# Attention probabilities, the last mixer part and x turned by 32-wide squares; the first two output blocks interleaved

## The reference

```
GLA(h) * silu(g_a)        gated linear attention, 4 heads
SSD(h, g_b)               state space mixer, 8 heads, gated and normed inside
MLA(h) * silu(g_c)        causal softmax attention, 4 heads of 192/128
DilatedSWA(h) * silu(g_d) softmax attention over dilated taps, 4 heads of 128
y = concat of the four, 256 x 2048;  x = x + y @ W_out (2048 x 2048)
```

## Time and profile before

| | |
|---|---|
| median of 3 runs | 809.48 us (809.12 to 809.54) |
| the profiled execution, its own time | 809.36 us |
| its span, first to last instruction | 807.6 us |
| busy: PE, DVE, ACT, POOL | 801.6, 616.7, 469.0, 100.5 us |
| granted TensorE clock | 0.999 |
| weights, queue q1 | 149.98 MB, 57.9% of 16 engines' span |
| POOL's queue, q0 | 18.95 MB, 8.6% |
| HBM over the span | 209 GB/s |

### The profile page before, as it was taken

The page is one execution under the profiler, slowest core; times in us unless marked ns, Lnnn a source line. Parts: engine busy times, 40 slices in busy tenths (PEclk is TensorE's granted clock), DMA queues, the critical chain, the costliest instruction groups (busy, mean ns, idle before and its releaser), DMA issues.

```text
span 807.6 us, 10773 instructions
## 1 busy us (share of the span) xinstructions
PE 801.6 (99%) x3940; PEld 678.9 (84%) x3940; DVE 616.7 (76%) x1084; ACT 469.0 (58%) x762; POOL 100.5 (12%) x154
## 2 busy tenths in 40 slices
PE   8999999999999999999999999999999999999998
PEld 5888888999887888888888888889998888888886
DVE  6678899887898776678964967988779988765452
ACT  6666544857865667443556465447777566663431
POOL 6200000030432211000000000002105231100000
PEclk9999999999999999999999999999999999999999
DMA  9966544576697977655676645365757979766663
GB/s 328 348 221 210 182 131 155 168 248 188 210 290 234 280 203 235 209 186 182 185 250 185 195 155 195 107 188 169 234 190 240 271 239 284 217 193 213 188 193 117
DMA packets 51348, 169.82 MB, mean 210 GB/s; under 512 B 6688, under 2 KB 7376, under 8 KB 51296
## 3 DMA queue, kind: packets, MB, share of 16 engines
q1 hardware_dynamic: 44736, 149.98, 57.9%
q0 software_dynamic: 6240, 18.95, 8.6%
q10 hardware_dynamic: 320, 0.21, 0.1%
HBM read 157.56 MB, written 11.55 MB: 209 GB/s over the span
## 4 chain that ended last, share of the span: by engine, by line
PE 91%; DVE 6%; issue 2%; DMA 1%; SPq 0%; ACT 0%; DVEq 0%
PE gemm L750 27%; PE gemm L741 27%; PE gemm L742 27%; DVE arena L1381 3%; DVE w_lo L1420 2%; PE pairs L917 1%; DMA raw<-in_weights_dram 1%; PE pairs L896 1%; PE pairs L891 1%; PE pairs L892 1%; PE pairs L862 1%; PE pairs L807 1%; DVE arena L1509 1%; PE pairs L931 1%; PE pairs L944 0%
## 5 line engine op out<-in xcount | busy, mean ns | idle before, releaser
L1420 DVE TENSOR_TENSOR w_lo<-raw,w_hi 128x1024 fp32r<-128x1024 f32 (+2 forms) x279 | 323.0, 1169 | 143.2 <-ACT w_hi L1046 142.3
L741 PE MATMUL gemm<-w_hi,a_hi 128*128 128x512 f32 (+2 forms) x1080 | 415.0, 384 | 0.8 <-ACT w_hi L1046 0.8
L742 PE MATMUL gemm<-w_hi,a_lo 128*128 128x512 f32 (+2 forms) x1080 | 408.9, 379 | 0.0
L1046 ACT ACTIVATE w_hi<-raw 128x1024 fp32r<-128x1024 f32 (+2 forms) x279 | 278.5, 1012 | 209.3 <-PE gemm L750 127.2
L750 PE MATMUL gemm<-w_lo,a_hi 128*128 128x512 f32 (+2 forms) x1080 | 278.4, 379 | 0.2
L741 PEld LDWEIGHTS gemm<-w_hi,a_hi 128*128 128x128 f32 x1080 | 202.8, 188 | 36.8 <-ACT w_hi L1046 1.7
L742 PEld LDWEIGHTS gemm<-w_hi,a_lo 128*128 128x128 f32 x1080 | 203.0, 188 | 33.4
L750 PEld LDWEIGHTS gemm<-w_lo,a_hi 128*128 128x128 f32 x1080 | 199.4, 188 | 36.7 <-DVE w_lo L1420 2.2
L634 POOL TENSOR_TENSOR st<-st,powers 128x4 f32<-128x4 f32 (+2 forms) x8 | 2.5, 309 | 365.5 <-ACT arena L1127 213.0
L1079 ACT ACTIVATE u<-gemm,st 128x512 f32<-128x512 f32 (+2 forms) x36 | 21.3, 646 | 15.3 <-PE gemm L750 15.3
L1381 DVE STREAM_TRANSPOSE arena<-u 32x256 f32<-32x256 f32 x64 | 27.9, 436 | 1.2
(11 more groups left out here) (215 smaller groups left out, 663.0 us busy)
## 6 DMA issues: line engine op xcount, KB each, us to landing
raw<-in_weights_dram SPq DMA_DIRECT2D x225, 512.0 KB, 4.2
raw<-in_weights_dram SPq DMA_DIRECT2D x38, 384.0 KB, 3.5
raw<-in_weights_dram SPq DMA_DIRECT2D x16, 344.0 KB, 3.5
y_squares<-arena POOLq DMA_DIRECT2D x6, 512.0 KB, 5.8
arena<-y_squares POOLq DMA_DIRECT2D x24, 128.0 KB, 5.8
x<-in_x_dram SPq DMA_DIRECT2D x4, 512.0 KB, 6.0
o<-ssd_rows SPq DMA_DIRECT2D x8, 256.0 KB, 5.3
param_rows<-in_params_dram SPq DMA_DIRECT2D x2, 904.0 KB, 8.0
```

The costliest lines, as they stand in the source:

```text
L741: pe.matmul(acc_t[t], a_hi[:, k, tok[t]], hi, start=k == 0, stop=False)
L742: pe.matmul(acc_t[t], a_lo[:, k, tok[t]], hi, start=False, stop=False)
L1046: A_(w_hi[:, g % SPLIT, 0:c], raw[:, g % RAW, 0:c], ACT.Copy).then_inc(hi_done, 1)
L1420: TT(w_lo[:, g % SPLIT, 0:c], raw[:, g % RAW, 0:c], w_hi[:, g % SPLIT, 0:c].bitcast(F32), ALU.subtract).then_inc(split_done, 1)
```

## The change

- `probs_T` and `yT` are gone from PE, with their four plus one jobs a layer. After `mla P i` and `dil P i` DVE makes squares of the probabilities (`probs_squares`, two transposes), POOL sends them out and back (384 KB each way), and ACT's `probs_T` reorders them into `PT`. The buffer is the finished `dq`/`dk` part of `u`, one token half for each i.
- The values go behind slots 98, 102, 107 and 112; ACT's copy to `PT` stands one slot on.
- `y 3` goes by squares as the other three.
- The stream visits output blocks 13 and 14 as six units of 13, six of 14, then the last two of 13 and of 14. Only those last need `yT 3`, whose copy moves to slot 125. The sums into x of the two blocks move to slots 128 and 130 (from 122 and 130).
- Quarters 0 to 2 of x go by squares (two DVE transposes each) at slots 129, 131 and 139; ACT's and DVE's splits read them in another order, DVE in two instructions per 128 features for one.
- POOL's list gets the new transfers in a fixed order.

```diff
+TAIL = UPB - 2
+FIRST_OUT = [U_OUT + b * UPB + k for k0, k1 in ((0, TAIL), (TAIL, UPB)) for b in range(2) for k in range(k0, k1)]
-for _n in range(UNITS):
+for _n in [*range(U_OUT), *FIRST_OUT, *range(U_OUT + 2 * UPB, UNITS)]:
...
-          "mla kv 1": KV_AT, "ssd Y": 76, "mla rT": 87, "mla S 0": 90, "mla PT 0": 93,
-          "mla S 1": 94, "mla O 0": 95, "mla PT 1": 97, "mla O 1": 99, "dil S 0": 99,
-          "dil PT 0": 102, "dil S 1": 103, "dil O 0": 104, "dil PT 1": 106, "dil O 1": 108,
-          "yT 3": 114}
+          "mla kv 1": KV_AT, "ssd Y": 76, "mla rT": 87, "mla S 0": 90,
+          "mla S 1": 94, "mla O 0": 98, "dil S 0": 99, "mla O 1": 102, "dil S 1": 103, "dil O 0": 107, "dil O 1": 112}
...
-Y_TURN = {1: 98, 0: 100, 2: 107}
-Y_SPLIT = [110, 112, 114, 117]
+Y_TURN = {1: 98, 0: 100, 2: 107, 3: 115}
+Y_SPLIT = [110, 112, 114, 125]
-X_NEXT = {N_SLOTS - 21: 0, N_SLOTS - 13: 1, N_SLOTS - 5: 2}
+X_NEXT = {N_SLOTS - 15: 0, N_SLOTS - 13: 1, N_SLOTS - 5: 2}
+X_UPDATE = {N_SLOTS - 16: N_INB, N_SLOTS - 14: N_INB + 1, N_SLOTS - 6: N_INB + 2}
...
+        for _i in range(2):
+            SQUARES[f"mla P {_i}"] = SQUARES[f"dil P {_i}"] = (u[:, _i, COL["dq"]:COL["dq"] + 768],) * 2 + ((94, 98)[_i],)
+        for _j, _n in zip(X_NEXT.values(), X_NEXT):
+            SQUARES[f"x {_j}"] = (u[:, 0, _j * 1024:(_j + 1) * 1024],) * 2 + (_n,)
...
                 squares_back(l, "ssd y")
                 squares_out(l, "dil q")
+                squares_out(l, "dil k")
+                squares_out(l, "mla P 0")
                 rsqrt("ssd rs", brs, bss)
-                squares_out(l, "dil k")
+                squares_back(l, "mla P 0")
                 squares_back(l, "dil q")
                 squares_back(l, "dil k")
-                for name in ("y 1", "y 0", "y 2"):
+                squares_out(l, "mla P 1")
+                squares_back(l, "mla P 1")
+                squares_out(l, "y 1")
+                squares_out(l, "dil P 0")
+                squares_back(l, "y 1")
+                squares_back(l, "dil P 0")
+                for name in ("y 0", "dil P 1", "y 2"):
                     squares_out(l, name)
                     squares_back(l, name)
 
+                squares_out(l, "y 3")
+                squares_back(l, "y 3")
+                if l + 1 < DEPTH:
+                    for j in range(3):
+                        squares_out(l, f"x {j}")
+                        squares_back(l, f"x {j}")
                 pool.wait_ge(*reached("dve", l)("yT 3"))
 
...
-                def yT(j):
-
-                    pe.wait_ge(*dve(f"y {j}"))
-                    ps = bank()
-                    for kk in range(4):
-                        for t in range(T):
-                            f = kk * P
-                            last = pe.transpose(ps[:, kk // 2, (kk % 2) * S + t * P:(kk % 2) * S + (t + 1) * P], o[:, j, t, f:f + P], ident)
-                    last.then_inc(*signal("pe", f"yT {j}"))
...
-                def probs_T(m, i):
-
-                    pe.wait_ge(*(act if m == "mla" else dve)(f"{m} P {i}"))
-                    ps = bank()
-                    for r in range(2):
-                        for c in range(3):
-                            last = pe.transpose(ps[:, r, c * P:(c + 1) * P], Pb[:, r, c * P:(c + 1) * P], ident)
-                    last.then_inc(*signal("pe", f"{m} PT {i}"))
...
                 def probs_T(m, i):
-                    act_.wait_ge(*pe(f"{m} PT {i}"))
-                    A_(PT[:, :, :], pair_of(f"{m} PT {i}")[:, :, 0:384], ACT.Copy).then_inc(*signal("act", f"{m} PT {i}"))
+                    act_.wait_ge(squares_in[f"{m} P {i}"], 16 * 4 * (l + 1))
+                    if (m, i) != ("mla", 0):
+                        act_.wait_ge(*pe(f"{m} O 0" if i else "mla O 1"))
+                    to, squares = PT.rearrange("p r (c i a) -> p i (r c) a", i=4, a=32), SQUARES[f"{m} P {i}"][1].rearrange("p (i x a) -> p i x a", i=4, a=32)
+                    A_(to, squares, ACT.Copy).then_inc(*signal("act", f"{m} PT {i}"))
...
-                                if n == slot(f"{m} PT {i}"):
+                                if n == slot(f"{m} O {i}", 1):
                                     probs_T(m, i)
...
+                    if l and i < len(X_NEXT):
+                        for t in range(T):
+                            hi, lo = (tokens(m[:, k, :])[:, t] for m in (a_hi, a_lo))
+                            last = v.scalar_tensor_tensor(lo, turned(i, k)[:, t], gain(l, k), hi.bitcast(F32), ALU.mult, ALU.subtract)
+                        continue
...
-                    if i:
-                        v.wait_ge(*pe(f"{m} PT {i - 1}"))
+                    if (m, i) != ("mla", 0):
+                        v.wait_ge(*me(f"{m} P 0 squares" if i else "mla P 1 squares"))
...
+                def probs_squares(m, i):
+
+                    v.wait_ge(*(act if m == "mla" else me)(f"{m} P {i}"))
+                    if (m, i) == ("mla", 0):
+                        v.wait_ge(*me("dil k squares"))
+                    to = SQUARES[f"{m} P {i}"][0].rearrange("p (f r c a) -> p r f c a", f=4, r=2, c=3)
+                    for r in range(2):
+                        last = v.transpose(to[:, r], Pb[:, r].rearrange("p (c f b) -> p f c b", c=3, f=4))
+                    last.then_inc(*sig(f"{m} P {i} squares"))
...
-                            turn(xturned[j], x[:, :, j * WB:(j + 1) * WB]).then_inc(*sig(f"x turn {j}"))
+                            turn_squares(SQUARES[f"x {j}"][0], x[:, :, j * WB:(j + 1) * WB].rearrange("p t (k c) -> p t k c", k=4)).then_inc(*sig(f"x {j} squares"))
...
                             gated(GD)
+                            y_squares(GD)
```

More of the change, by code:

```diff
@@ L249 @@
         "mla cT, ssd Y, mla rT, "
-        "mla S 0, mla PT 0, mla S 1, mla O 0, mla PT 1, mla O 1, dil S 0, dil PT 0, dil S 1, dil O 0, "
-        "dil PT 1, dil O 1, yT 3",
+        "mla S 0, mla S 1, mla O 0, dil S 0, mla O 1, dil S 1, dil O 0, dil O 1",
     "act":
-        "x rs sum, evac 0, evac 1, gla lr, gla abs, gla exp, gla ln, evac 2, gla E 0, gla E 1, "
-        "gla E 2, gla cross, gla E 3, gla E 4, evac 3, gla E 5, gla E 6, gla E 7, evac 4, ssd abs, ssd exp, "
-        "ssd eA, ssd ln, conv 3 1, gla rs sum, conv 3 0, evac 5, ssd silu 1, "
@@ L256 @@
[L256 removed]
[3 rows of a table removed]
[L260 to L267 removed]
[3 rows of a table removed]
+        "x rs sum, evac 0, evac 1, gla lr, gla abs, gla exp, gla ln, evac 2, gla E 0, gla E 1, gla E 2, gla cross, gla E 3, "
@@ new lines @@
+        "gla E 4, evac 3, gla E 5, gla E 6, gla E 7, evac 4, ssd abs, ssd exp, ssd eA, ssd ln, conv 3 1, gla rs sum, conv 3 0, "
+        "evac 5, ssd silu 1, mla crs sum, ssd gcol, ssd silu 0, evac 6, ssd exp 0, mla cT, ssd xD, ssd exp 1, mla q 0, evac 7, "
+        "mla q 1, mla rs 0 sum, mla kv 0, mla kv 1, mla rs 1 sum, dil rs 0 sum, evac 8, dil rs 1 sum, mla qT, evac 9, mla rT, "
+        "mla P 0, ssd rs sum, mla P 1, evac 10, mla PT 0, dil q, dil P 0, mla PT 1, evac 11, dil P 1, dil PT 0, yT 0, yT 1, "
@@ new lines @@
+        "dil PT 1, yT 2, evac 12, yT 3",
+    "dve":
+        "pad, gla turn, gla dots, gla zero 0, gla zero 1, gla la, gla scan 0, gla scan 1, gla D 0, gla D 1, gla W 0, gla D 2, "
+        "gla W 1, gla D 3, gla W 2, gla merge 1, gla D 4, gla W 3, gla merge 2, gla D 5, gla W 4, gla merge 3, gla D 6, gla W 5, "
+        "gla merge 4, gla D 7, gla W 6, gla merge 5, gla W 7, gla merge 6, ssd turn, gla merge 7, ssd dt0, ssd dt, ssd la, "
+        "conv 1 0, conv 1 1, gla o, conv 1 2, conv 1 3, conv 1 4, conv 1 5, ssd row, conv 0 0, conv 0 1, conv 0 2, conv 0 3, "
+        "conv 0 4, conv 0 5, ssd CB, mla cn, ssd x squares, ssd E 0, mla cT, ssd E 1, ssd M 0, ssd xdt, ssd M 1, mla n 0 0, "
+        "mla n 0 1, ssd yT, mla q squares, mla n 1 0, ssd y squares, mla n 1 1, mla rope products, mla rope, mla k squares, "
+        "dil n 0 0, dil n 0 1, dil n 1 0, dil n 1 1, dil rope 0 products, dil rope 0, dil rope 1 products, dil rope 1, gated 1, "
+        "mla max 0, mla nmax 0, dil q squares, dil k squares, mla P 0 squares, mla max 1, mla nmax 1, y 1, mla P 1 squares, "
[3 rows of a table added]
@@ L386, in build @@
         rows = o[:, 2:4].rearrange("p g t c -> p (g t c)").rearrange("p (h s) -> p h s", h=SSD_H)
-        xturned = [u[:, 0, j * 1024:(j + 1) * 1024].rearrange("p (k s) -> p k s", k=4) for j in range(3)]
         SQUARES = {}
@@ L470, in build @@
         squares_out_done, squares_in = ({name: sem(name.replace(" ", "_") + end) for name in SQUARES} for end in ("_squares_out", "_squares_in"))
-        squares_d = {name: nc.dram_tensor(name.replace(" ", "_") + "_squares", (P, 4 * S), F32, kind="Internal").ap() for name in SQUARES}
+        squares_d = {name: nc.dram_tensor(name.replace(" ", "_") + "_squares", SQUARES[name][0].shape, F32, kind="Internal").ap() for name in SQUARES}
         setup_chain = sem("setup_chain")
@@ L970, in stages @@
                             scores("dil", i, (dqT, dkT), False)
```

(15 more changed lines are left out.)

39 lines of the change are left out of this document (13 added, 26 removed), and 9 rows, old and new, of the table ORDER.

## The result

| | before | after |
|---|---|---|
| median | 809.48 us (3 runs, 809.12 to 809.54) | 827.57 us (4 runs, 825.31 to 831.77) |
| ratio, with its 95% interval | | 1.0226 [1.0208, 1.0243] |
| the profiled execution, its span | 809.36, 807.6 us | 831.77, 829.9 us |
| granted TensorE clock | 0.999 | 0.988 |

The change makes the kernel 2.3% slower. The profiled execution is the slowest of its four, 4.2 us over their median. A fourth run of the kernel before was disturbed (1002.99 us), as was one each in experiments 6 and 9; medians and ranges leave these out.

The account below looks back on a forecast made before the run. PE was taken to bound the kernel (91% of the chain): 809.36 - 7.18 of PE work + 16.0 of stall (8.0 a layer) = 818.2 us, forecast 818. The 8-in-10 range was 801 to 826, the forecast's own 812 to 824.

Parts of the forecast that it names:

- the larger gap: PE in front of slot 115: `y 2` comes back late, ACT's copy `yT 2` waits, PE stands 6.0 us a layer.
- What PE loses: On PE, both layers: transposes of probabilities (four jobs of 0.67 a layer) and of `yT 3` (0.91) go, 7.18 us saved.
- The edits at nothing: `y 3` by squares, the interleaved output blocks and x by squares: all hidden, costing nothing.
- `dil S 0`: PE at slot 99's end: dil k comes back 0 to 1.1 us late, taken as 0.5 a layer.
- `mla P 1`: Its transfer lands at 684.4, its use is behind slot 102 at 683.7: taken as hidden, up to 2 us if not.
- the three outs at 6.5 us each: POOL's late waits for outs of `y 0`, `dil P 1`, `y 2`: between 4.8 (idle queue) and 9.6 (behind backs), 6.5 taken.
- (c): Rival: queue full throughout, outs at 9.2 us, 2 us from `mla P 1`, relieved while ACT waits; 824 to 830 us; chance 0.13.
- The forecast 1.5 at the next `w_lo`: PE behind slot 115's start: DVE has 6.0 us of work where PE wants `w_lo` in 4.5, another 1.5 us a layer.
- (a): Rival: all hidden, each out taking 4.8 us, `y 2` back just at its deadline; 802.2 us; chance 0.20.
- (b): Rival: a short stall, outs at 5.2 to 5.8 us, `y 2` 2 to 4 us late; 804 to 812 us; chance 0.17.

Follow-up runs that it names:

- experiment 6: Kernel after with only the out of `y 0` moved ahead of out `dil P 0`, its backs behind those of `dil P 0`: 819.08 us, ratio 1.0106.
- experiment 9: Kernel after, same transfers in the same order, but `mla P 1`, `dil P 0`, `dil P 1` and all four y parts carry half their columns: 810.43 us, ratio 1.001.
- experiment 12: Kernel after with early backs `mla P 0` before dil q and dil k, late backs `dil P 0`, `y 0`, `y 1`, earlier outs: 805.15 us, ratio 0.994.
- experiment 3: Kernel after with the probabilities turned on PE again and values where they stood before; `y 3`, x by squares and interleaving kept: 807.6 us, ratio 0.9976.
- experiment 11: Repeat, for its trace, of the kernel after with half the columns in `mla P 1`, `dil P 0`, `dil P 1` and the y transfers: 811.16 us, ratio 1.0012.
- experiment 8: Kernel before with eight more table loads on ACT ahead of `yT 2`, 10.2 us, in both layers, no transfer added: 832.55 us, ratio 1.0284.
- experiment 2: Kernel after with the first two output blocks streamed as four, four, two, two, two, two units and `yT 2` copied at slot 122: 809.69 us, ratio 1.0.
- experiment 4: Kernel after with only POOL's order changed, outs earlier and backs behind them, same bytes: 805.59 us, ratio 0.9952.
- experiment 5: Kernel after with POOL's outs issued earlier and the stream of four, four, two, two, two, two units: 805.72 us, ratio 0.9941.
- experiment 7: Kernel after with the four, four, two, two, two, two stream, `mla O 1` behind slot 103, and outs moved earlier in POOL's order: 805.03 us, ratio 0.9948.
- the four best versions: Experiment 4, experiment 5, experiment 7 and experiment 12, all with POOL's transfers reordered against the kernel after: 805.0 to 805.7 us.

## Why the prediction was wrong

The direction was right, and so was the mechanism of the larger gap, the one in front of slot 115; the size was not: 818 forecast, 827.6 measured, outside the range. Step by step.

**What PE loses: right.** 7.18 us forecast. With the same instructions as the kernel after and hardly a gap, experiment 12 has PE busy 794.8 us against 801.6, 6.8 less.

**The edits at nothing: right**, by experiment 3. **`dil S 0`:** 0.5 us late forecast, 0.51 and 0.71 measured. **`mla P 1`** was hidden, as taken.

**The step that failed: the three outs at 6.5 us each.** They took 13.0, 7.6 and 3.8, so 24.4 together for 19.5. A value between the rows (4.8 and 9.6) was the wrong way to choose, for each row has its own queue in front of it. Counted in bytes, outs with weights beside them agree. In the kernel before 0.52 MB behind nothing took 4.76 us, and 0.52 MB behind a set of backs of 0.52 MB took 9.62: 110 and 109 GB/s. In the kernel after `y 0` has 0.52 + 0.39 MB of backs ahead and 0.52 of its own, 1.44 MB in 13.03 us, 111 GB/s. Halved, in experiment 11, 0.72 MB in 6.39 us, 113. `dil P 1` behind the backs of `y 0`: 0.92 MB in 7.61 us, 120. At 110 GB/s the prediction's own rows give 13.1 for `y 0` and 8.3 for `dil P 1`, by an estimate that counts all that was issued just before, though part of it had already moved (the queue itself moved 1.23 MB in those 13.03 us, 94 GB/s).

The rate is not the queue's own, for it hangs on what the weights take. By the same count `mla P 1` had 1.05 + 0.39 = 1.44 MB, as many as `y 0`, and took 6.67 us, 216 GB/s; ACT stood 2.97 us for dil q there, and over 680.5 to 683.5 hardly any weights moved (0.01 MB). `y 2` took only 3.8, as ACT had stood for `yT 0` until 721.85 and no weights moved from 722 to 728: what the prediction said under (c) of a stall that relieves the queue. One of its two rows for an idle queue was none, either: in the 5.74 us the queue moved 0.82 MB, 0.3 of it the last of dil k's backs.

The Trainium skill, DMA: Bandwidth & Descriptors, section on SWDGE, HWDGE and iDMA, says that software and hardware DMAs feed different internal queues of each DMA engine, which the engine serves in turn. Equal turns would give POOL's queue about half of the bytes, an estimate. The trace doesn't bear that out for `y 0`, where it got a third (1.23 MB to 2.56), and no run here shows the serving itself. The rule that the Trainium skill gives on the same page, section on the anatomy of one DMA by the GpSimd path, 2.0 us plus bytes over 436 GB/s, is 3.2 us for 512 KB. The out of `y 2` in the kernel after, with no weights beside it at first, came near it (3.5 us to landing, 3.2 in the first layer); that of `y 0` took 12.7.

**The chain as a whole.** The lateness of `y 2` follows step by step. From the out of `y 0` to the copy `yT 2` I forecast 31.4 us (690.4 to 721.8). Measured are 39.0 (700.27 to 739.29): 4.9 more for the three outs, 2.2 more from the backs of `y 2` to the copy (9.7 for 7.5), 0.5 more to issue a set of backs that came in two pieces. From the start of the copy to PE's first matmul it is 6.05 us, 5.95 forecast. PE in turn wanted slot 115 at 745.34 - 8.01 = 737.3, 37.1 us after the out of `y 0`, where I had 31.3: its own gap at slot 111 gave 3.3, and 2.1 came from the out of `dil P 0`, most of which passed under the issue of the backs of `y 1` (5.1 us between the outs of `dil P 0` and `y 0` for 7.2). 39.0 + 6.05 - 37.1 = 8.0 late, for 6.0 forecast.

**Not priced: `y 0` itself.** I followed `y 0` only as something that delays `y 2`. ACT stood 8.37 us for it, and PE lost 2.67 + 0.59 at slot 111 (2.48 + 0.58 in the first layer). This comes from the same mis-sized term: at 6.5 and 7.5 `y 0` would have been back 14.0 us after its out, and ACT came to it after 13.2 (713.48 - 700.27), so it would have stood 0.8 us; it came back after 21.6. The forecast 1.5 at the next `w_lo` behind slot 115 didn't appear in the kernel after; the likely reason is that PE ran at the low clock and came late itself. In experiment 11, where the long gap is missing, it stands as 1.45 and 0.99.

**Not priced: the clock behind the gap.** The prediction put it at nothing, without a reason. PE is busy 801.0 us in the kernel after and 794.8 in experiment 12 for the same matmuls: 6.2 us. Experiment 8 shows the same without any change of transfers, 5.2 us for two gaps.

**The sum again**, by spans: 807.6 - 6.8 + 22.9 more idle time + 6.2 at the low clock = 829.9. Forecast were 16.0 of stall and nothing for the clock. Of the 13.6 us between 818.2 and 831.77, then, some 7 are stall and 6 the clock. PE's gaps in both layers, by place: 15.2 in front of slot 115 for 12.0 forecast, 6.3 at slot 111 for none, 1.2 at `dil S 0` for 1.0, and none at the `w_lo` behind slot 115 for 3.0, an error the other way that hid a part of the rest. The median lies 4.2 us lower, as the length of the stall changes from run to run (825.31 to 831.77, and 805.69 to 813.94 in experiment 2, against 809.12 to 809.54 before).

**The rivals.** (a), all hidden, fell: it needed 4.8 for each out. (b) fell too. (c), the full queue, is nearest by its time (824 to 830), and its picture of full DMA engines is right for 699 to 711 us; but it has the outs at 9.2 throughout and `mla P 1` late, and neither is so. Experiment 4 is as fast as it is with every byte in place and the engines full from 670 to 694 us: order decided, and bytes set the price of a bad order. In the small its picture holds: each of experiments 5, 7 and 12, meant to free the last late piece, came out at its rival's 804 to 807, with another piece late.

**Open.** What holds the four best versions at 805 in place of 802.2: the one profiled execution of each shows gaps of 0.3 to 2.7 us, at different pieces. Why POOL's queue got a third of the bytes for `y 0` and more than half for `mla P 1` is seen only in part (the weights paused), and why the clock fell at one gap of 2.77 us and not at one of 2.87 (last section) is open as well.

## What to carry to other kernels

Price a transfer on a serial queue by all the bytes in front of it over the queue's rate under load, not by the time of a transfer alone; two rows with known bytes gave that rate here. It holds only while the other queue keeps its share: where the weights paused, the same count of bytes took half the time. Then follow each piece in the chain to its own reader, not only the last one. Issue the outs when their data are ready and put the backs where something has to wait anyway: an out that waits for its producer, or a wait for a landing, holds up every out behind it that is ready.
